# Decode attention over a paged cache: block transposes on VectorE, scores in 32x32 array tiles, page loads from two queues

## The reference, cut to what matters

```python
past_ckv = cache_ckv[page_table].reshape(B, -1, KV_LORA)     # B=8, 32 pages of 128 tokens
past_kr = cache_krope[page_table].reshape(B, -1, QK_ROPE)
s_past = (einsum('blhc,btc->bhlt', q_lat, past_ckv)
          + einsum('blhr,btr->bhlt', q_rope, past_kr)) * ATTN_SCALE
p = softmax(concatenate([s_past, s_new], -1), -1)
o_lat = einsum('bhlt,btc->blhc', p[..., :T], past_ckv) + einsum('bhls,bsc->blhc', p[..., T:], ckv)
return einsum('blhc,chd->blhd', o_lat, w_uv)
```

## Time and profile before

| what | us |
|---|---|
| median of three runs | 1611.43 |
| profiled execution | 1615.35 |
| its span | 1613.4 |
| decode block in it, first work to last | 571.80 to 800.42 |
| TensorE busy in 577 to 800 us | 177.22 of 223 |
| VectorE busy in 577 to 800 us | 71.13 of 223 |
| ScalarE busy in 577 to 800 us | 46.39 of 223 |

### The profile page before, as it was taken

One profiled execution on the slowest core, in us unless ns is written; L12 is line 12 of the kernel. 1 busy time (PEld: TensorE's weight loads), 2 busy tenths in 40 slices (PEclk: granted clock), 3 DMA queues, 4 the chain that ended last, 5 costly groups with the idle time before them and its releaser, 6 DMA issues. The chain is left out here.

```text
span 1613.4 us, 24089 instructions
## 1 busy us (share of the span) xinstructions
PE 1383.7 (86%) x8142; PEld 1118.7 (69%) x8142; DVE 950.3 (59%) x1422; ACT 663.6 (41%) x902; POOL 175.5 (11%) x254
## 2 busy tenths in 40 slices
PE   4989999896788888777679993799999999936997
PEld 4989999785454465555458872688888888825886
DVE  4457566653677633333244445688888888745653
ACT  5222344320566522212132111677777777633221
POOL 6000211051000010000001000000000000012310
PEclk9999999796899989989879995899999999967999
DMA  5121211475984046555272220469656999935410
GB/s 182 31 78 40 69 53 54 159 224 160 322 305 112 1 127 182 164 169 169 65 240 104 105 92 26 171 245 357 247 219 217 333 404 405 378 141 206 157 66 39
DMA packets 131791, 275.02 MB, mean 170 GB/s; under 512 B 23601, under 2 KB 58930, under 8 KB 131378
## 3 DMA queue, kind: packets, MB, share of 16 engines
q1 hardware_dynamic: 116706, 217.16, 40.4%
q0 software_dynamic: 11824, 45.11, 7.7%
q10 hardware_dynamic: 3168, 11.54, 1.8%
HBM read 214.34 MB, written 58.38 MB: 169 GB/s over the span
## 5 line engine op out<-in xcount | busy, mean ns | idle before, releaser
L399 PE MATMUL pb<-xH,wH 128*128 128x344 f32 x432 | 142.5, 330 | 26.4 <-DVE wL L858 10.9
L400 PE MATMUL pb<-xL,wH 128*128 128x344 f32 x432 | 140.1, 324 | 0.0
L401 PE MATMUL pb<-xH,wL 128*128 128x344 f32 x432 | 140.0, 324 | 0.0
L2507 DVE TENSOR_TENSOR downL<-raw_down,downH 128x2048 fp32r<-128x2048 f32 x44 | 98.9, 2288 | 44.5 <-ACT downH L2409 39.4
L2409 ACT CAST gateH<-raw_gate 128x2048 fp32r<-128x2048 f32 x44 | 83.8, 1910 | 66.8 <-PE pb L2342 40.8
L2507 DVE TENSOR_TENSOR gateL<-raw_gate,gateH 128x2048 fp32r<-128x2048 f32 x44 | 100.5, 2287 | 15.8 <-ACT gateH L2409 15.8
L399 PEld LDWEIGHTS pb<-xH,wH 128*128 128x128 f32 x432 | 83.0, 192 | 28.9 <-issue 10.8
L2507 DVE TENSOR_TENSOR upL<-raw_up,upH 128x2048 fp32r<-128x2048 f32 x44 | 100.3, 2282 | 1.0 <-ACT upH L2409 1.0
L1477 PE MATMUL pb<-cst,pages 128*128 128x128 f32 x512 | 73.7, 309 | 28.7 <-DMA pages<-in_cache 27.2
L1477 PEld LDWEIGHTS pb<-cst,pages 128*128 128x128 f32 x512 | 66.8, 160 | 37.0 <-DMA pages<-in_cache 32.0
L1646 DVE COPY pgT<-pb 128x512 f32<-128x512 f32 x64 | 41.9, 687 | 79.4 <-PE pb L1477 78.9
(11 more groups left out here) (447 smaller groups left out, 3279.1 us busy)
## 6 DMA issues: line engine op xcount, KB each, us to landing
pages<-in_cache SPq DMA_DIRECT2D x256, 144.0 KB, 2.4
raw_gate<-in_w_gate SPq DMA_DIRECT2D x32, 1024.0 KB
raw_up<-in_w_up SPq DMA_DIRECT2D x32, 1024.0 KB, 8.2
raw_down<-in_w_down SPq DMA_DIRECT2D x32, 1024.0 KB, 8.5
y_d<-yzero POOLq DMA_DIRECT2D x4, 4096.0 KB, 31.0
y_d<-yo ACTq DMA_DIRECT2D x22, 512.0 KB, 3.9
wraw_p<-in_w_blk SPq DMA_DIRECT2D x18, 512.0 KB, 3.5
xa<-in_x_all SPq DMA_DIRECT2D x9, 512.0 KB, 3.7
```

Source lines behind the costliest of these rows:

```text
L399: pe.matmul(out, wh, xh, start=first, stop=False)
L400: pe.matmul(out, wh, xl, start=False, stop=False)
L401: return pe.matmul(out, wl, xh, start=False, stop=last)
L2507: dve.tensor_tensor(part(low_[w], c), part(raw[w], c), part(high[w], c).bitcast(F32), ALU.subtract).then_inc(S(w + "_low"), 1)
```

## The change

- Pages: a ring of 11 groups of 8 pages (`RING3`) in place of three buffers of 32. The group with number `at` = 4b + g may be loaded once batch (at - 11) // 4 is weighed. Of each group from 4 on, SP reads the numbers of pages 0 to 3 and loads them, and GpSimd (`pool`) those of pages 4 to 7.
- Turning: VectorE turns each group with one `transpose` in 32x32 blocks, 128 x 2304 values (SBUF to SBUF). TensorE's transposes of pages, the copies out of PSUM and GpSimd's copies go away.
- Scores: for each of the 9 blocks of 32 latent or rotary rows, four row strips x two column strips (32x32 tiles), 8 stationary and 256 moving columns: 144 products a batch, in two halves (groups 0 and 1, then 2 and 3). The row strips write to four PSUM banks, which are single: scores(b) waits for the exp of b-1.
- The exp runs once over 1024 values (before 256). The probabilities are turned in 8 products with the identity's columns.
- VectorE's order: turn(b+1, 0), turn(b+1, 1), largest(b), row_sums(b-1), row_bounds(b), turn(b+1, 2), turn(b+1, 3). TensorE's: scores(b), turn_probs(b-1), largest_row(b), first half of weigh(b-1), bound_column(b), second half.
- The result of a batch is scaled on ScalarE and kept (`o_all`); it is turned for all batches at the end. `w_uv` is loaded when the last scores are done.

```diff
-        def load_pages(sp, b, n, groups=range(4)):
...
+        SHARE = {'sp': (0, 4), 'pool': (4, 4)}
+        def load_pages(eng, name, at, first, some):
+            found = nc.values_load_multi_w_load_instructions(
+                pt_sb[0:1, bass.ds(8 * at + first, some)], engines=(ENGINE[name],), min_val=0, max_val=cache.shape[0] - 1)[1]
+            for m, page in enumerate(found):
+                eng.dma_start(group_pages(at)[:, first + m, :], cache[bass.ds(page, 1), :, :].rearrange("a p w -> (a p) w")).then_inc(page_sw[at % RING3] if name == "pool" else page_in[at % RING3], 16)
+        def load_share(eng, name, at):
+            if at >= RING3:
+                eng.wait_ge(S("spv_mm"), (at - RING3) // 4 + 1)
+            load_pages(eng, name, at, *SHARE[name])
...
+            for j in range(NJ - 1):
                 for h in range(H):
+                    last = pe.matmul(pb[0:32, 6, (j * H + h) * NB:(j * H + h + 1) * NB], ukt[:, h, 32 * j:32 * j + 32], qd[:, h, :], start=True, stop=True)
...
+            def scores(b):
+                if b:
+                    pe.wait_ge(S("sexp_rdy"), 2 * b)
+                for half in range(2):
+                    pe.wait_ge(S("pgT_rdy"), 4 * b + 2 * half + 2)
+                    for j in range(NJ):
+                        for r in range(4):
+                            for g in (2 * half, 2 * half + 1):
+                                at = slice(32 * r, 32 * r + 32)
+                                last = pe.matmul(pb[32 * g:32 * g + H, r, 0:256], q4[at, b, j, :], pgT[at, 8 * g:8 * g + 8, 32 * j:32 * j + 32],
+                                                 start=j == 0, stop=j == NJ - 1, skip_group_check=True, tile_position=(32 * r, 32 * g))
+                    last.then_inc(S("past_mm"), 1)
...
+            def turn_probs(b):
...
+                for x in range(8):
+                    last = pe.matmul(pb[:, 4, 32 * x:32 * x + 32], pexp[:, x, :, :].rearrange("p g t -> p (g t)"), heads, start=True, stop=True)
...
+            for b in range(1, NB + 1):
+                if b < NB:
+                    scores(b)
+                turn_probs(b - 1)
+                if b < NB:
+                    largest_row(b)
+                weigh(b - 1, range(0, PAGES // 2))
+                if b < NB:
+                    bound_column(b)
+                weigh(b - 1, range(PAGES // 2, PAGES))
...
+            def turn_pages(b, g):
+                pages_in(dve, 4 * b + g)
                 if b:
+                    dve.wait_ge(S("past_mm"), 2 * b - 1 + g // 2)
+                dve.transpose(pgT[:, 8 * g:8 * g + 8, :], group_pages(4 * b + g)).then_inc(S("pgT_rdy"), 1)
...
+            for b in range(NB):
+                if b + 1 < NB:
+                    turn_pages(b + 1, 0)
+                    turn_pages(b + 1, 1)
+                largest(b)
                 if b:
+                    row_sums(b - 1)
                 row_bounds(b)
                 if b + 1 < NB:
+                    turn_pages(b + 1, 2)
+                    turn_pages(b + 1, 3)
```

More of the change, by code:

```diff
@@ L1442, in _ @@
         def _(sp):
[L1443 to L1449, removed]
+            for at in range(4, GRPS):
+                load_share(sp, "sp", at)
+            sp.wait_ge(S("past_mm"), 2 * NB)
+            sp.dma_start(wuv, w_uv.rearrange("(c p) n -> p c n", p=P)).then_inc(S("uv_in"), 16)
         @block.tensor
@@ L1461, in _ @@
[L1461 to L1509, removed]
@@ L1552, in latent @@
-            def latent(b):
-                pe.wait_ge(S("o_rdy"), b + 1)
-                for c in range(2):
-                    last = pe.matmul(pb[:, 7, 2 * KL - 64 + c * H:2 * KL - 64 + (c + 1) * H], o_sb[:, c * P:(c + 1) * P], sel32, start=True, stop=True,
-                                     skip_group_check=True)
-                last.then_inc(S("olat_mm"), 1)
-            scores(0, 0)
-            for b in range(NB):
-                bounds(b)
-                if b + 1 < NB:
-                    scores(b + 1, (b + 1) % 2)
-                weigh(b, b % 2)
-                latent(b)
@@ new lines, in weigh @@
+            def weigh(b, some):
+                if some[0] == 0:
+                    pe.wait_ge(S("pT_rdy"), b + 1)
+                    if b:
+                        pe.wait_ge(S("o_rdy"), b)
+                for x in some:
+                    q = x % 4
+                    last = pe.matmul(pb[32 * q:32 * q + H, 7, 0:KL], pT[b % 2][:, x % 8, x // 8, :], group_pages(4 * b + x // 8)[:, x % 8, 0:KL], start=x < 4,
+                                     stop=x >= PAGES - 4 and q > 0, skip_group_check=True, tile_position=(0, 32 * q))
+                if some[-1] == PAGES - 1:
+                    pe.wait_ge(S("pTn_rdy"), b + 1)
+                    pe.matmul(pb[0:H, 7, 0:KL], pTn[:, :], ckvn[:, :], start=False, stop=True, skip_group_check=True,
+                              tile_position=(0, 0)).then_inc(S("spv_mm"), 1)
@@ new lines, in _ @@
+            pe.wait_ge(S("q4_rdy"), 2)
+            pe.wait_ge(S("newT_rdy"), 2)
+            pe.wait_ge(S("b_zero"), 2)
+            scores(0)
+            pe.wait_ge(S("small_zero"), 5)
+            largest_row(0)
+            bound_column(0)
+            for b in range(1, NB + 1):
[8 more added lines that the diff above has]
+                weigh(b - 1, range(PAGES // 2, PAGES))
```

292 lines of the change are left out of this document (122 added, 170 removed).

## The result

The changed kernel takes 1593.45 us (median of 6, 1589.42 to 1600.54) against 1611.66 of the kernel before (1607.24 to 1613.49): a ratio of 0.9894, 95% interval 0.9872 to 0.9916. That is 1.1% faster, clear of the noise but under 2%. Predicted were 1588 us, between 1569 and 1620.

The account below looks back on a forecast made before the run. SP's issuing of page loads was taken to bound the block, 28 us a batch. First weighing at 616, five turns of 25.2 and a last part of 34.2 end it at 776.2 instead of 800.4: 1588 us, range 1569 to 1620.

Parts of the forecast that it names:

- What bounds the kernel before: Decode block: SP's issuing of page loads bounds it, 28 us a batch, with TensorE close behind at 23.2 busy.
- T = 4.6 us and the landing: Page loads: GpSimd reads and issues its four pages of a group in 4.6 us; pages land 2.0 after the issue.
- rival 2: GpSimd's page loads: reading page numbers costs by the call, a group takes 6.0 us, the whole 1609; chance 12%.
- The turn, 25.2 us: One turn of the page ring: three group loads, landing, transpose, largest value, row and weigh sum to 25.2 us a batch.
- Slack of the scores: Scores on TensorE beside the ring: a half takes 4.3 us at 30 ns a record, leaving 3.9 us of slack.
- Ends: Block's start and finish around five turns: first weighing done at 616, last part 34.2 us, end at 776.2 instead of 800.4.
- G(0): Moment when batch 0 is weighed and ring slots may be loaded again: 616 us with a slow clock.
- G(5): Moment when batch 5 is weighed, which frees group 31: 742 us, with 34.2 us from there to the end.
- 1, GpSimd held by VectorE: GpSimd's load issues are held during VectorE's block transposes, up to 5.2 us a turn: 1618 us; chance 14%.
- 3, transposes at two cycles: VectorE's page transposes take two cycles a value, 5.1 us each: +33, 1620 us; chance 7%.
- 4, row strips: Scores on TensorE: row strips don't overlap, 104 ns a record, a turn of 37.8 us: near 1700 us; chance 5%.
- 5: Loads at the transfer's pace, 4.15 us a group, and quick VectorE transposes of 1.7 us: 1571 us; chance 22%.

Follow-up runs that it names:

- e1: Kernel before, with only the page loads from batch 1 on shared, four of each group by SP and four by GpSimd: 1574.82 us, ratio 0.9787.
- e10: e7 with all eight pages of every group issued by SP again: 1615.24 us, ratio 1.002 to the kernel before.
- e3: Changed kernel with a ring of 10 groups in place of 11: 1617.91 us, ratio 1.004 to the kernel before.
- e4: Changed kernel with the row-strip loop outermost in the scores, so only two 32x32 tiles work at a time: 1862.67 us (one run).
- e7: Changed kernel with the weigh between the halves of the scores and two groups' slots freed after half a weigh: 1554.18 us, ratio 0.966.
- e11: Changed kernel with the slots of a batch's first two groups freed after the first half of its weighing: 1580.27 us, ratio 0.9817.
- e6: Changed kernel with the weighing of the batch before moved between the two halves of the scores: 1564.82 us, ratio 0.9721.
- e8: Changed kernel with 22 added products, their result unread, between the halves of the scores of batches 1 to 7: 1608.47 us, ratio 0.9989.

## Why the prediction came out right

*What bounds the kernel before*: right. e1 and e10 show it from both sides: sharing the issuing alone takes 36 us away, and all the rest without it, even in the better order, nothing. TensorE was close behind, as said: with SP out of the way a batch took 22.1 us, 1 less than the 23.2 that it had been busy.

*T = 4.6 us and the landing*: their sum was right, by luck; two terms missed in opposite directions. The issue took 537 ns at the least and 577 at most in 112 issues, with 0.05 us between two: four pages in 2.31 us, the reading of four numbers 1.35 more, 3.66 a group. So I had the reading right (1.43; it goes by the number, rival 2 is out) and a page by 0.2 too dear. In the mean of the five turns the third group's issue ended 11.7 us behind the weighing (13.8), and its transpose began 4.3 us after that, between 3.3 and 5.6 (2.0): together 16.0 against 15.8. I had put GpSimd's issue in place of the transfer, and left the landing at the 2.4 of the earlier trace rows, where one queue fed the DMA engines; now the median is 3.7 from GpSimd's queue. While the pages come over, the DMA engines are full (stretch after):

```profile
674.00:688.00 14.00, 7.40 (x212) 3.96 (x196) 5.77 (x3) 0.00 (x0) 7.85 (x15) 0.76 0.96 299
```

At 299 GB/s a group of 1.18 MB takes 3.9 us, more than its issuing. The 24 pages from 673.20 on were there at 687.39; the first 8 took 6.05 us of it, the other two groups 4.1 each in the mean. e3 gives nearly the same from outside, 4 to 4.5 us for one group. By the Trainium skill ("DMA: Bandwidth & Descriptors", "Issuing engines are not separate DMA queues") two issuers bring no bandwidth; the trace agrees in the main: 299 GB/s over these 14 us against 284 in the best slice of the earlier trace rows, and GpSimd's pages came in larger packets (last section), whose part in the difference no run shows apart.

*The turn, 25.2 us*: measured 25.95 over the same five. Loads and landing 16.0 (15.8), transpose 2.58 (2.6), largest 1.8 (1.95), row, weigh and bound 5.6 (4.85). The miss is the low clock in half a weigh, which I had named with up to 1.7 and added nothing for: it came in three of the five turns, 1.1 to 1.4 us each. In the other two the last term was 4.7 and the turn 24.2. That was the choice most against the evidence: the earlier trace rows show it after a wait of 2.7 us, and I had worked out a longer one.

*Slack of the scores*: right. Half of them took 4.09 us (144 records, started 26 ns apart, (4.09 - 0.38) / 143) where I had 4.3. The second half took 5.1 to 5.4 for 128, in part at the low clock, in each of the six turns; VectorE's largest value waited for them once, at the start (5.8 us). GpSimd's loads stood for 9.2 to 12.8 us a turn (10.6 to 14.1 with the reading) and not 7, since a group is issued in 3.66.

*Ends*: G(0) 616.6 (616). The last part, from G(5), 37.2 us (34.2); 2.0 of the miss lie in its first step, 8.6 us to landed pages where I had 6.6. Sum of the misses: 0.6 + 5 x 0.75 + 3.0 = 7.3 us, the 783.55 against 776.2; 4.4 of it came back by the blocks around, which nobody had forecast (1593.95 against 1591). That is luck too: the block, which is all that the sum is about, became 17 us shorter and not 24.

*Rivals.* 1, GpSimd held by VectorE: out. The 577 ns are the longest issue of 112, with 32 transposes of 2.58 us among them. The rule of the Trainium skill ("SBUF — State Buffer", "Who interferes with whom") left it to the mode for an operation with one input (for two inputs in SBUF it speaks of GpSimd's reads alone, which I had put too widely); that this transpose doesn't hold them is what this trace adds. 2: out. 3, transposes at two cycles: out, 2570 ns in the mean over 32. 4, row strips: out by the 26 ns, and dearer than I had it (e4). 5: its first half came, since the pages moved at 3.9 to 4.1 us a group, its 4.15 or better; but the landing was longer and the transposes weren't quick, so its 1571 did not. In the chances, some 5% (the forecast's upper end) are counted both under faster and under same, and slower gets that much too little.

What I did not see is that a better kernel lies on both sides of this one: the sharing alone (e1), and the change in another order (e7). I had written that the loads stand still in each turn and drew nothing from it; it was the fault of the change. The ring of 11 holds less than three batches, and a slot comes free only when the scores of the next batch are done. Freed half a weigh earlier it is 12 to 13 us (e11), with the weigh between the halves 28 (e6), with both 38 (e7).

## What to carry to other kernels

When an issue queue is relieved, find what the loads wait for next: here a slot, freed by work that had no need to be so late. Where a ring of buffers closes a loop over several engines, write its turn as a sum and ask of each term whether it has to lie between the freeing and the filling; here an earlier weighing and an earlier freeing together gave another 38 us, twice what the whole change gave. And run the parts of a change alone: here one part held twice the gain of the whole.

## What the runs showed of the hardware

- VectorE's transpose of 128x2304 float32 values in 32x32 blocks takes 2.58 us, 1.12 ns a value of a partition, SBUF to SBUF, and GpSimd's DMA issues beside it aren't lengthened (537 to 577 ns in 112).
- The same page makes other packets on the two queues. In 664 to 700 us some 16 pages came by each (the DMA view after: packets, MB, share of the engines; q1 is SP's, q0 GpSimd's):

```profile
DMA packets 3079, 4.82 MB, mean 134 GB/s; under 512 B 512, under 2 KB 2560, under 8 KB 3072
...
q1 hardware_dynamic: 2304, 2.36, 21.8%
q0 software_dynamic: 768, 2.36, 19.7%
```

  That is 144 packets a page from SP and 48 from GpSimd. 512 of all are small ones, 16 for each of the 32 pages; taken as 16 on either queue, a page is 128 packets of 1.15 KB from SP and 32 of 4.6 KB from GpSimd (2048 lie between 512 B and 2 KB and 512 between 2 and 8 KB, which is what 16 pages of each make). GpSimd's take slightly less of the engines' time for the same bytes.
- Eight 32x32 tiles of the array in work start a record of 256 columns every 26 ns. Two start one every 167 ns, and there the granted clock stays at the 1.2 GHz level although TensorE never stands (e4). In e8 it fell to that level in the middle of unbroken work as well. In these two runs busy time by itself didn't keep the clock.
